# Feed-forward up products by feature: the order of 32 matmuls within a chunk of weights

## The reference, cut to what matters

```
gate, up = split(rmsnorm(x) @ w_in)       # 256x1024 @ 1024x5632
h = (silu(gate) * up) @ w_out             # 256x2816 @ 2816x1024
```

## Time and profile before

| | |
|---|---|
| median of three runs | 2083.86 us (2080.04 to 2084.1) |
| profiled execution, its own time | 2083.83 us |
| its span, first to last instruction | 2082.4 us |
| granted clock of TensorE, mean | 0.996 |
| PE busy | 2052.8 us, 99% of the span, 10644 matmuls |
| DVE, ACT busy | 69%, 57% |
| share of the ending chain in L559, L561 | 21%, 11% |

### The profile page before, as it was taken

The page is one execution under the profiler, slowest core; times in us unless marked ns, Lnnn a source line. Parts: engine busy times, 40 slices in busy tenths (PEclk is TensorE's granted clock), DMA queues, the critical chain, the costliest instruction groups (busy, mean ns, idle before and its releaser), DMA issues.

```text
span 2082.4 us, 27111 instructions
## 1 busy us (share of the span) xinstructions
PE 2052.8 (99%) x10644; PEld 1732.1 (83%) x10644; DVE 1434.0 (69%) x2054; ACT 1181.0 (57%) x1905; POOL 64.8 (3%) x101
## 2 busy tenths in 40 slices
PE   8999999999999999999999999999999999999998
PEld 6877888888887788888888888878888888887887
DVE  5987756764688775766576557776775766588763
ACT  5547566553546656655465446755554655586552
POOL 0001100000000200000000000000000000010000
PEclk9999999999999999999999999999999999999999
DMA  7572444545555244455554545615555555545553
GB/s 246 198 249 95 148 162 150 196 187 182 196 197 214 83 161 162 158 186 186 182 209 182 198 176 185 225 58 194 191 190 188 189 195 187 197 157 192 183 197 125
DMA packets 54782, 372.56 MB, mean 179 GB/s; under 512 B 7351, under 2 KB 7647, under 8 KB 11008
## 3 DMA queue, kind: packets, MB, share of 16 engines
q1 hardware_dynamic: 49392, 356.54, 47.0%
q10 hardware_dynamic: 4752, 12.70, 1.8%
q0 software_dynamic: 512, 1.57, 0.4%
HBM read 369.46 MB, written 1.34 MB: 178 GB/s over the span
## 4 chain that ended last, share of the span: by engine, by line
PE 93%; ACT 3%; DVE 2%; DMA 1%; issue 0%; SPq 0%; DVEq 0%; ACTq 0%
PE ps L559 21%; PE ps L513 17%; PE ps L517 17%; PE ps L514 17%; PE ps L561 11%; PE ps L697 2%; PE ps L590 1%; PE ps L681 1%; PE ps L630 1%; PE ps L930 1%; PE ps L646 1%; DMA ring<-in_w 1%; ACT S L2353 0%; DVE ring_lo L1349 0%; PE ps L1173 0%; ACT upper_w L2215 0%
## 5 line engine op out<-in xcount | busy, mean ns | idle before, releaser
L1349 DVE TENSOR_TENSOR ring_lo<-ring,upper_w 128x1024 fp32r<-128x1024 f32 x435 | 526.3, 1224 | 212.5 <-ACT upper_w L2215 211.4
L2215 ACT CAST upper_w<-ring 128x1024 fp32r<-128x1024 f32 x435 | 449.2, 1050 | 290.4 <-DMA ring<-in_w 166.5
L514 PE MATMUL ps<-ring_lo,nT_pair 128*128 128x512 f32 (+1 forms) x1000 | 388.6, 389 | 0.0
L513 PE MATMUL ps<-upper_w,nT_pair 128*128 128x512 f32 (+1 forms) x864 | 344.4, 399 | 3.2 <-DVE ring_lo L1349 3.2
L561 PEld LDWEIGHTS ps<-nT_pair,ring_lo 128*128 128x128 f32 x1920 | 261.9, 190 | 18.8
L517 PE MATMUL ps<-upper_w,nT_pair 128*128 128x512 f32 (+1 forms) x696 | 271.6, 390 | 0.0
L561 PE MATMUL ps<-nT_pair,ring_lo 128*128 128x256 f32 x1920 | 267.7, 282 | 0.0
L514 PE MATMUL ps<-ring_lo,z_hi 128*128 128x512 f32 x624 | 242.9, 389 | 0.0
L559 PE MATMUL ps<-nT_pair,upper_w 128*128 128x512 f32 x960 | 240.8, 393 | 0.0
L514 PEld LDWEIGHTS ps<-ring_lo,nT_pair 128*128 128x128 f32 x1000 | 189.7, 190 | 36.6 <-issue 0.5
L517 PE MATMUL ps<-upper_w,tT_lo 128*128 128x512 f32 (+1 forms) x528 | 204.9, 388 | 0.0
(11 more groups left out here) (380 smaller groups left out, 2886.6 us busy)
## 6 DMA issues: line engine op xcount, KB each, us to landing
ring<-in_w SPq DMA_DIRECT2D x338, 1024.0 KB, 4.8
big<-in_gains ACTq DMA_DIRECT2D x7, 512.0 KB, 4.5
z<-in_mem ACTq DMA_DIRECT2D x2, 1024.0 KB, 7.2
big<-skew POOLq DMA_DIRECT2D x8, 192.0 KB, 7.1
x<-in_x SPq DMA_DIRECT2D x2, 512.0 KB, 6.3
ring<-in_w SPq DMA_DIRECT2D x2, 512.0 KB, 6.8
PTs<-skew ACTq DMA_DIRECT2D x1, 1024.0 KB, 4.4
big<-skew ACTq DMA_DIRECT2D x1, 1024.0 KB, 7.9
```

The lines of the kernel that those rows point to most:

```text
L513: PE.matmul(out, hi, w_hi, start=start, stop=False)
L514: PE.matmul(out, hi, w_lo, start=False, stop=False)
L1349: V.tensor_tensor(ring_lo[:, q % RING, cols], ring[:, q % RING, cols], upper(n).bitcast(F32), ALU.subtract).then_inc(*lo_cut.up(h))
L2215: A.copy(upper(n), ring[:, q % RING, part * HALF:(part + 1) * HALF]).then_inc(*hi_cut.up(h))
```

## The change

The two halves of a chunk are taken together. First come the sixteen matmuls with the upper weights of both halves, each half after a wait for ACT's rounding (`hi_cut`) alone. Then come the sixteen with the lower weights, each half after the wait for DVE's subtraction (`lo_cut`). The signal `half_used` and the call of `beside` stay behind the lower matmuls of their half. The number, the shapes and the operands of the matmuls are the same.

```
-            for c, h in enumerate(W.span[seg]):
-                w_hi, w_lo = weights(h)
-                tiles = [(2 * c + k, i, slice(k * BLK + i * P, k * BLK + (i + 1) * P)) for k in range(2) for i in range(4)]
-                for f, i, cols in tiles:
-                    PE.matmul(ps[:, base + i, :], w_hi[:, cols], nT_pair[:, :, f, :], start=(f == 0), stop=False)
-                for f, i, cols in tiles:
-                    m = PE.matmul(ps[:, base + i, 0:T], w_lo[:, cols], nT_hi[:, f, :], start=False, stop=(f == KT - 1))
-                m.then_inc(*half_used.up(h))
-                if beside:
-                    beside(c)
+            tiles = [(k, i, slice(k * BLK + i * P, k * BLK + (i + 1) * P)) for k in range(2) for i in range(4)]
+            halves = list(enumerate(W.span[seg]))
+            for chunk in (halves[0:2], halves[2:4]):
+                for c, h in chunk:
+                    PE.wait_ge(*hi_cut.at(h))
+                    for k, i, cols in tiles:
+                        PE.matmul(ps[:, base + i, :], upper(W.halves[h][2])[:, cols], nT_pair[:, :, 2 * c + k, :], start=(c == 0 and k == 0), stop=False)
+                for c, h in chunk:
+                    w_hi, w_lo = weights(h)
+                    for k, i, cols in tiles:
+                        m = PE.matmul(ps[:, base + i, 0:T], w_lo[:, cols], nT_hi[:, 2 * c + k, :], start=False, stop=(2 * c + k == KT - 1))
+                    m.then_inc(*half_used.up(h))
+                    if beside:
+                        beside(c)
```

## The result

The changed kernel takes 2085.70 us in the median of 20 runs (2082.34 to 2089.32), the one before 2082.69 in 20 runs beside it (2079.93 to 2084.63). The ratio is 1.0015, interval 1.0009 to 1.0021: slower by 1.9 to 4.4 us, 3.1 at the middle. Forecast were +2.6 us and 2086.4.

The account below looks back on a forecast made before the run. PE, busy 99% of the span, was taken to bound the kernel, so only matmul pace and new PE waits count. From 2083.83 us, -2.4 for order and +5.0 for the wait gave 2086.4, range 2081.4 to 2089.0.

Parts of the forecast that it names:

- part 1: PE's matmul order: merging runs of eight into sixteen saves 0.020 us per pair, 120 pairs, 2.4 us in all.
- The split into 0.027 lost and 0.007 won: After a change of shape, the first 512-column run pays 0.027 us extra; the 256-column run is 0.007 us shorter.
- Rival B: The order saves nothing and the wait at `up2` stands alone: 2088.8 us, chance 0.10.
- part 2: Moved first_gated delays `up2`'s third bank: 0.68 us wait, 0.83 us a block with restart, +5.0 us over six blocks.
- X: Start of first_gated's transposes, from which the chain is timed: third bank free at X + 2.08, PE ready at X + 1.40.
- The restart: PE resuming at `up2`: 0.05 to 0.06 us signal plus 0.10 slow first step; upper bound 1.0 us a block, wait included.
- part 3: Shifted weight needs, slot release, added waits, and ACT and DVE work behind the transposes, all costed at nothing.
- a wait for a cut at the upper matmuls: Sign against the prediction: a wait for `hi_cut` (ACT) showing at the upper matmul line, L559.
- The push of ACT and DVE behind the transposes: DVE's gates come about 1.2 us later, L1585 near 366.8; 7 us left before `up3` needs the banks.
- A (no wait): No wait at `up2`, the chain of copies stays hidden, the order's gain stands alone: 2081.4 us, chance 0.10.
- C (short matmuls can't hold 0.12 us): Sixteen 256-column matmuls run PE's queue dry and slow to 0.163 us each, losing 41 us: 2127, chance 0.03.
- "The same": Whole kernel's time not distinguishable from before, within 0.2%, about 4.2 us: chance 0.77.

Follow-up runs that it names:

- gated_mid: Changed kernel with `beside(2)` called ahead of the fourth half's upper matmuls: 2079.85 us, ratio 0.9988 to the kernel before.
- thirtytwo: All 32 upper matmuls of a unit, then all 32 lower, root_rows and first_gated together behind the third upper run: 2078.49 us, ratio 0.9986 to the kernel before.
- fours: Kernel before with upper and lower matmuls alternating in runs of four in place of eight: 2085.48 us, ratio 1.0011.
- snake: Halves in order upper, lower, lower, upper, each finished before the next, first_gated not moved: 2079.61 us, ratio 0.9981 to the kernel before.
- late_gated: Kernel before, runs of eight kept, only first_gated's transposes moved behind the fourth half's upper run: 2087.56 us, ratio 1.0021.
- late_wait: Changed kernel, each unit waiting for its third and fourth bank only ahead of their first matmul: 2082.66 us, ratio 1.0004 to the kernel before.
- gated_early: Changed kernel with first_gated called right behind root_rows, at the end of the first chunk: 2080.25 us, ratio 0.9987 to the kernel before.
- snake_joined: snake with first_gated called right behind root_rows: 2079.66 us, ratio 0.9991 to the kernel before.
- ones: Kernel before with one 512-column and one 256-column matmul in turn: 2090.78 us, ratio 1.0037.

## Why the prediction was right, step by step

**The order (part 1, -2.4 us).** Confirmed. gated_mid has it alone and shows -2.2 for 114 pairs, which is 0.019 a pair; thirtytwo shows -3.5 for 180. The split into 0.027 lost and 0.007 won is also what the starts in the trace give. One ground named for it does not hold. The stretch of the earlier trace rows does not change bank at every step: `up0` goes by tokens and puts all its matmuls of one half of the tokens into one bank, so only the last of the twenty goes to another. That the surplus belongs to what ran before and not to the place is shown by the first run of a block (3.62 us for sixteen in place of 3.66), by the second sixteen of thirtytwo and by fours instead. Rival B is refuted by gated_mid, snake and thirtytwo, whose intervals all lie below 1. With it goes the reading that part 1 would be worth nothing by the formula in the Trainium skill ("TensorE: Matmul & The Clock Gate", section "Back-to-back issue gap"), which has only a matmul's own columns in it and which the page gives for an isolated matmul: in this stream of loads and matmuls the steps are 227 ns and not 216, and they depend on the matmuls before.

**The wait (part 2, +5.0 us).** The place, the chain and the bank are confirmed by late_gated and late_wait, and the 0.68 us of lateness can be read off again: PE is ready at X + 1.39 (in snake) and the bank free at X + 2.08. The restart was mis-sized. The prediction took 0.05 to 0.06 us for the signal from the earlier trace rows, and it is 0.20. The first step was taken 0.10 us longer than usual and is about 0.07: the sixteen matmuls behind the wait take 362.52 to 366.25, 3.73 us in place of 3.66.

```profile
366.25 0.40 PE L565 MATMUL ps<-nT_pair,ring_lo 128*128 128x256 f32 x2
```

Together 0.69 + 0.20 + 0.07 = 0.96 us; late_gated measures (113.35 - 112.38) = 0.97 us a block in place of 0.83, 5.9 us over six blocks in place of 5.0. The prediction had 1.0 as its upper bound for just this case, several waits at the head of `up2` that need a separate step, and chose the lower value because the earlier trace rows was the nearest row. In the trace that row has no separate wait instruction directly ahead of its load, while `up2` has two. This 0.9 us is the difference between the forecast of +2.6 and the +3.4 of the blocks; the order, at -2.5 between late_gated and the changed kernel, takes 0.1 back.

**The edits at nothing (part 3).** The prediction named a wait for a cut at the upper matmuls as a sign against it. The profile seems to show one, but that is the bracket discussed above, and in late_wait `up2` starts before that cut ends. Apart from the six waits, no idle time of PE or its loads stands at the two lines, neither after the change nor in gated_mid or snake. The push of ACT and DVE behind the transposes cost nothing more: counted from the start of the block, L1585 of before ended at 365.52 - 350.80 = 14.72 us and its like in the changed kernel, L1589, at 364.97 + 0.69 - 349.86 = 15.80, so 1.1 us later where 1.2 was forecast, and PE has no idle time at `up3`. Two sentences of part 3 are off without effect on the sum. The first half's lower weights are needed 1.8 us later (3.66 - 1.84) and not 3.6, and the added waits do not all ride on weight loads, for L559 stands 60 times as an instruction of its own.

**The rivals.** A (no wait) is refuted by the six waits. C (short matmuls can't hold 0.12 us) is refuted by the 32 of thirtytwo at 0.120 each.

**The range and the chances.** 2085.70 lies inside 2081.4 to 2089.0. "The same", the likeliest case, holds for the middle of the ratio, 1.0015; its interval reaches to 1.0021, just past the edge of 0.2%. The size came out 0.5 to 0.8 us above the forecast, and it isn't luck that it came so near: both terms were measured alone, and the one that was off by 0.9 us stayed inside its bounds.

**What the change could have been.** The order is worth 2.2 to 3.5 us in the blocks and the side effect costs 5.9. Moving one call, or using the order of snake, gives the gain without the loss. snake (ratio 0.9981) and thirtytwo (0.9986, the shortest blocks) were both measured faster than the kernel before, by 0.1 to 0.2%; their intervals overlap, so which is faster as a whole isn't settled.

## What to carry to other kernels

When a loop body is regrouped, look first at the things that are hooked into it. The new order was worth 0.02 us for each pair of runs, but a hook that fed a PSUM bank moved from sixteen matmuls ahead of the bank's next use to eight, past the 2.08 us that its chain of copies needs. Compare for each hook the work left behind it with the length of what it starts. And measure a small change by the stage that it touches: here that separated 0.02 us a pair, where whole runs scatter by 4 us.

## What the runs showed of the hardware that was not expected

The hybrid stage, whose code is the same in all kernels, took 294.50 us in the profiled execution of before, 292.88 in that of the changed kernel and 291.30 in that of snake, steps of 1.6 us. It goes with TensorE's granted clock. Between 1230 and 1250 us two stretches of ten stand at 0.83 in the kernel before, that is in part at 1.2 GHz in place of 2.4, in the changed kernel only one is low (0.84), in snake none. (A further stretch at 0.83, from 1380 to 1390 us, is in all three and makes no difference between them; PE was busy for only 7.58, 7.58 and 6.46 us of the ten ahead of it.) First before, then the changed kernel, then snake (stretch; length, busy time of PE, PEld, DVE, ACT, POOL; clock; DMA share; GB/s):

```profile
1230.00:1240.00 10.00, 10.00 (x60) 8.82 (x58) 1.23 (x1) 1.07 (x2) 0.00 (x0) 0.83 0.27 107
1240.00:1250.00 10.00, 10.00 (x43) 8.24 (x43) 4.72 (x4) 5.75 (x7) 0.00 (x0) 0.83 0.62 224
```

```profile
1230.00:1240.00 10.00, 10.00 (x70) 9.12 (x68) 1.53 (x2) 1.73 (x3) 0.00 (x0) 0.99 0.36 139
1240.00:1250.00 10.00, 10.00 (x39) 8.16 (x39) 5.18 (x5) 6.19 (x7) 0.00 (x0) 0.84 0.72 252
```

```profile
1230.00:1240.00 10.00, 10.00 (x70) 9.11 (x69) 1.77 (x2) 2.46 (x3) 0.00 (x0) 1.00 0.23 79
1240.00:1250.00 10.00, 10.00 (x46) 8.27 (x45) 6.62 (x6) 6.12 (x8) 0.00 (x0) 1.00 0.79 307
```

PE's row says busy throughout, and for 29.97 of the 30.00 us ahead of 1230. But what it did there is not the usual work. Twice in this place it runs 24 matmuls of only 24 columns, 0.11 us apart. In the kernel before the first series is followed by 512-column steps of 0.43 us in place of 0.23:

```profile
1231.24 0.17 PE L513 MATMUL ps<-upper_w,nT_pair 128*128 128x24 f32 x1
...
1233.72 0.26 PE L517 MATMUL ps<-upper_w,nT_pair 128*128 128x24 f32 x1
...
1235.36 0.63 PE L517 MATMUL ps<-upper_w,nT_pair 128*128 128x512 f32 x1
1235.79 0.63 PE L513 MATMUL ps<-upper_w,nT_pair 128*128 128x512 f32 x1
```

In all eleven profiled executions the falls between 1230 and 1250 us stand behind such a series: behind both in before, late_gated, gated_early and thirtytwo, behind one in the changed kernel, gated_mid, snake_joined, fours and ones, behind none in snake and late_wait. So such a series can be followed by a fall and need not be. The order doesn't decide it, for gated_mid and gated_early share the order and differ here; what does isn't shown.

This is part of the scatter between runs, and it is as large as the effects studied here: the runs of the kernel before near 2080 us have a mean clock of 0.998, those near 2084 us one of 0.996. Unexpected too were the surplus behind transposes that is no cost, and the two rhythms of alternating single matmuls, both told above.
